# Long convolution between the gated products of a one-core transformer kernel

## What is computed

```python
proj = u @ w_in[i]
y_a = conformer_conv_branch(proj[..., OFF_CONV:OFF_Z], ...) @ w_conv_out[i]
y_b = ssd_branch(...) @ w_ssd_out[i]
y_c = swa_branch(...) @ w_attn_out[i]
gates = sigmoid(proj[..., OFF_GATE:IN_COLS] + gate_bias[i])
merged = gates[0] * y_a + gates[1] * y_b + gates[2] * y_c

def conformer_conv_branch(u, dw_w, dw_b, ln_g, ln_b):
    a, gate = jnp.split(u, 2, axis=-1)
    h = a * jax.nn.sigmoid(gate)
    h = causal_depthwise_conv(h, dw_w, dw_b)   # 31 taps, per feature
    h = layer_norm(h, ln_g, ln_b)
    return jax.nn.silu(h)
```

## Time and profile before

| | us |
|---|---|
| median of 3 runs | 2835.9 |
| lowest, highest | 2833.11, 2838.72 |
| the profiled execution | 2840.97 |
| its span on the core | 2838.9 |

### The profile page before, as it was taken

One profiled execution on the slowest core, in us unless ns is written; L12 is line 12 of the kernel. 1 busy time (PEld: TensorE's weight loads), 2 busy tenths in 40 slices (PEclk: granted clock), 3 DMA queues, 4 the chain that ended last, 5 costly groups with the idle time before them and its releaser, 6 DMA issues.

```text
span 2838.9 us, 53058 instructions
## 1 busy us (share of the span) xinstructions
PE 2747.1 (97%) x22084; PEld 2404.2 (85%) x22084; DVE 1436.5 (51%) x2761; ACT 1185.8 (42%) x2115; POOL 1473.2 (52%) x809
## 2 busy tenths in 40 slices
PE   7999999988889999999999999999999999999999
PEld 5888888767778888889888897899998898898999
DVE  3777226645554666504666124443174776612570
ACT  3222235334444322224222236644445665555553
POOL 2444434443323444443444433388885476597797
PEclk9999999999999999999999999999999999999999
DMA  6565323210001455433555326365564343354465
GB/s 271 188 209 201 106 88 97 92 60 3 3 4 32 149 183 186 150 95 122 190 171 182 111 76 123 102 198 187 171 186 134 97 149 120 103 180 149 141 194 164
DMA packets 105974, 380.98 MB, mean 134 GB/s; under 512 B 11367, under 2 KB 16648, under 8 KB 104456
## 3 DMA queue, kind: packets, MB, share of 16 engines
q1 hardware_dynamic: 87304, 310.47, 35.2%
q10 hardware_dynamic: 18432, 67.12, 6.7%
HBM read 373.34 MB, written 4.19 MB: 133 GB/s over the span
## 4 chain that ended last, share of the span: by engine, by line
PE 89%; DVE 4%; POOL 3%; ACT 3%; issue 2%; DMA 1%; SPq 0%; DVEq 0%; ACTq 0%
PE bank L233 24%; PE bank L234 24%; PE bank L235 24%; POOL weights_lo L226 2%; PE bank L1075 2%; PE upper_banks L233 1%; PE upper_banks L234 1%; PE upper_banks L235 1%; PE upper_banks L1880 1%; PE upper_banks L1863 1%; PE bank L1172 1%; PE bank L1854 1%; PE upper_banks L1091 1%; PE upper_banks L1052 1%; PE upper_banks L1202 1%
## 5 line engine op out<-in xcount | busy, mean ns | idle before, releaser
L226 POOL TENSOR_TENSOR weights_lo<-weights_landing,weights_hi 128x1024 fp32r<-128x1024 f32 x554 | 1339.3, 2424 | 1152.5 <-ACT weights_hi L216 1151.5
L216 ACT ACTIVATE weights_hi<-weights_landing 128x1024 fp32r<-128x1024 f32 x554 | 587.3, 1061 | 1162.7 <-PE bank L235 1048.9
L233 PE MATMUL bank<-normed_hi,weights_lo 128*128 128x256 f32 (+1 forms) x2776 | 926.7, 334 | 3.0 <-DVE normed_lo L736 1.7
L234 PE MATMUL bank<-normed_lo,weights_hi 128*128 128x256 f32 (+1 forms) x2776 | 919.2, 331 | 0.0
L235 PE MATMUL bank<-normed_hi,weights_hi 128*128 128x256 f32 (+1 forms) x2776 | 917.7, 331 | 0.0
L233 PEld LDWEIGHTS bank<-normed_hi,weights_lo 128*128 128x128 f32 x2776 | 522.8, 188 | 69.3 <-issue 4.4
L235 PEld LDWEIGHTS bank<-normed_hi,weights_hi 128*128 128x128 f32 x2776 | 522.9, 188 | 56.3
L234 PEld LDWEIGHTS bank<-normed_lo,weights_hi 128*128 128x128 f32 x2776 | 523.0, 188 | 55.9
L233 PE MATMUL bank<-hidden_hi,weights_lo 128*128 128x256 f32 (+1 forms) x1026 | 340.8, 332 | 0.0
L234 PE MATMUL bank<-hidden_lo,weights_hi 128*128 128x256 f32 (+1 forms) x1026 | 340.1, 331 | 0.0
L235 PE MATMUL bank<-hidden_hi,weights_hi 128*128 128x256 f32 (+1 forms) x1026 | 339.7, 331 | 0.0
(11 more groups left out here) (473 smaller groups left out, 3711.7 us busy)
## 6 DMA issues: line engine op xcount, KB each, us to landing
weights_landing<-w_up SPq DMA_DIRECT2D x176, 512.0 KB, 3.6
ada_rows<-w_ada_rows ACTq DMA_DIRECT2D x128, 512.0 KB, 4.4
weights_landing<-w_down SPq DMA_DIRECT2D x88, 512.0 KB, 3.5
weights_landing<-w_dn SPq DMA_DIRECT2D x33, 512.0 KB, 3.6
weights_landing<-w_mlp_up SPq DMA_DIRECT2D x32, 512.0 KB, 3.6
weights_landing<-w_mlp_down SPq DMA_DIRECT2D x32, 512.0 KB, 3.5
weights_landing<-w_gate SPq DMA_DIRECT2D x24, 512.0 KB, 3.5
weights_landing<-w_xbc SPq DMA_DIRECT2D x24, 512.0 KB, 3.5
```

What stands on the lines that cost most here:

```text
L216: k.nc.scalar.activation(k.WH[:, u % SLOTS, :], k.W[:, u % LANDS, :], ACT.Copy).then_inc(*k.AC.mark(("unit hi", u)))
L226: k.nc.gpsimd.tensor_tensor(k.WL[:, u % SLOTS, :], k.W[:, u % LANDS, :], k.WH[:, u % SLOTS, :].bitcast(F32), ALU.subtract).then_inc(*k.PO. ...
L233: nc.tensor.matmul(out, ll, rh, start=start, stop=False, skip_group_check=True)
L234: nc.tensor.matmul(out, lh, rl, start=False, stop=False, skip_group_check=True)
```

## The change

The gated products now use four banks (0 to 3) in turn. The convolution uses bank 7 alone. Its steps stand between the products: 6 steps behind the second product, 10 behind each of the third to seventh, 150 behind the last, then two after each of nine parts of the query projection and none after its last two. That makes 6 + 50 + 150 + 18 = 224 steps, seven tiles, ahead of the attention; one tile stays behind it. Each convolution tile waits for its own product only. The value projection no longer waits for four tiles of the convolution, and the attention's second output waits for tile 6 in place of tile 4. Nothing is computed differently.

```diff
@@ window_project_pe
-        pe.wait_ge(*k.DV.after("conv", 3))
@@ spread_heads_pe, outputs
-            pe.wait_ge(*k.DV.after("conv", CONV_APART))
+            pe.wait_ge(*k.DV.after("conv", KT - 2))
@@ long_conv
-        y = k.B[7 if at == CONV_APART else 6 + at % 2][:, 0:LAT]
-        dve.wait_ge(*k.DV.after("glu", "ev", KT - 1))
+        y = k.B[7][:, 0:LAT]
+        dve.wait_ge(*k.DV.after("glu", "ev", at))
@@ glu_pe
-    freed = lambda n: None if n < 8 else k.AC.after("glu", "sig", (n - 8) // 2) if n % 2 else k.DV.after("glu", "ev", (n - 8) // 2)
-    linear(k, pe, "glu", "w_glu", 2 * KT, KT, both2(k), LAT, freed, norm_ready(k, "norm mix"), first=4, banks=8)
+    freed = lambda n: None if n < 4 else k.AC.after("glu", "sig", (n - 4) // 2) if n % 2 else k.DV.after("glu", "ev", (n - 4) // 2)
+    linear(k, pe, "glu", "w_glu", 2 * KT, KT, both2(k), LAT, freed, norm_ready(k, "norm mix"), first=4)
@@ glu_dve
+        if 1 <= n < KT - 1:
+            take(conv, 10 if n > 1 else 6)
@@ gates_pe
-                       k.AC.after("glu", "sig", KT - 4 + n // 2) if n % 2 else k.DV.after("glu", "ev", KT - 4 + n // 2))
+                       k.AC.after("glu", "sig", KT - 2 + n // 2) if n % 2 else k.DV.after("glu", "ev", KT - 2 + n // 2))
@@ dve_program
-    glu_dve(k, dve)
     conv = long_conv(k, dve)
-    take(conv, 4 * (CONV + 1))
-    window_project_dve(k, dve, attn, lambda n: take(conv, 3 if n < KT + 2 else 2))
+    glu_dve(k, dve, conv)
+    take(conv, 150)
+    window_project_dve(k, dve, attn, lambda n: take(conv, 2 if n < KT + 1 else 0))
...
-    take(conv, 3 * (CONV + 1))
+    take(conv, CONV + 1)
```

More of the change, by code:

```diff
@@ L2065 @@
 CONV = 31
-CONV_APART = 4
 def both2(k):
@@ L2117, in glu_act, with glu_dve @@
                 act.wait_ge(*k.DV.after("glu", "ev", n // 2 - 2))
-            k.nc.scalar.activation(k.sigs[:, n // 2 % 2, :], k.B[n % 8][:, 0:LAT], ACT.Sigmoid).then_inc(*k.AC.mark(("glu", "sig", n // 2)))
-def glu_dve(k, dve):
+            k.nc.scalar.activation(k.sigs[:, n // 2 % 2, :], k.B[n % 4][:, 0:LAT], ACT.Sigmoid).then_inc(*k.AC.mark(("glu", "sig", n // 2)))
+def glu_dve(k, dve, conv):
     for n in range(KT):
         dve.wait_ge(*k.AC.after("glu", "sig", n))
-        k.nc.vector.tensor_tensor(k.gl[:, n, :], k.sigs[:, n % 2, :], k.B[2 * n % 8][:, 0:LAT], ALU.mult).then_inc(*k.DV.mark(("glu", "ev", n)))
+        k.nc.vector.tensor_tensor(k.gl[:, n, :], k.sigs[:, n % 2, :], k.B[2 * n % 4][:, 0:LAT], ALU.mult).then_inc(*k.DV.mark(("glu", "ev", n)))
+        if 1 <= n < KT - 1:
+            take(conv, 10 if n > 1 else 6)
 def gates_pe(k, pe):
     freed = lambda n: (k.AC.after("gates", "ev", n - 4) if n >= 4 else
-                       k.AC.after("glu", "sig", KT - 4 + n // 2) if n % 2 else k.DV.after("glu", "ev", KT - 4 + n // 2))
+                       k.AC.after("glu", "sig", KT - 2 + n // 2) if n % 2 else k.DV.after("glu", "ev", KT - 2 + n // 2))
     linear(k, pe, "gates", "w_gate", 24, KT, both2(k), LAT, freed)
```

## The result

| | before | with the change |
|---|---|---|
| median of 20 runs, us | 2836.6 | 2839.63 |
| lowest, highest | 2830.76, 2843.52 | 2835.16, 2847.57 |
| span of the profiled execution | 2838.9 | 2837.0 |

The ratio is 1.0014, with a 95% interval from 1.0008 to 1.0021: 2 to 6 us slower, some 4 us, which is inside the 0.2% taken as no change. A second series of 7 runs of the change, with 29 of the kernel before beside them, gave a ratio of 1.0026 (1.0015 to 1.0037), some 7 us; the two intervals overlap between 1.0015 and 1.0021. The forecast was +4.4 us and 2840.3 us.

What follows compares the result with a forecast made beforehand. PE was taken as the bound, busy 97% of the span with 89% of the chain that ended last. Terms 4.9 + 2.3 - 2.8 = +4.4 us gave a median of 2840.3 us, range 2835.0 to 2845.0.

Steps and rivals of the forecast that it cites:

- The wait: Gated products: with four banks PE stops before the fifth tile until the first product is done, +4.9 us (4.5 to 5.2).
- The chain: Gated products: weight DMA, weight copy, table load of 1.28 us and sigmoid set the first product's end, about 2041.3.
- The clock behind it: Gated products after PE's stop: 5.2 us at 1.2 GHz, losing 0.45 per microsecond, +2.3 us (0 to 2.8).
- the rival in which it holds: Gated products: the clock holds through PE's stop, sum +2.1 us, 2838.0 us; chance 15%.
- Ten steps between products, 150 under the gates: Gated products and gates: convolution steps fit, 5.55 us within 5.65 and 3.3 us left under the gates; cost 0.
- The attention's start: Seventh reciprocal to first maximum: seven fewer multiply-adds stand between, -2.8 us (-2.3 to -3.4).
- The walk: Attention's start, step by step from the seventh reciprocal at 2182.86: first maximum at 2186.4 in place of 2189.22.
- One tile behind the attention: Behind the attention: DVE reaches the xbc convolution 32.7 us earlier and waits for PE; gain 0.
- The slower rival: Gated products: the lower clock lasts 13.7 us behind the stop, costing 6.2 us, sum +8.3, 2844.2 us; chance 12%.
- The faster rival: Attention's start runs at the full clock, up to 6.2 us less, sum -1.8, 2834.1 us; chance 5%.

Runs made afterwards that it cites:

- early table load: The changed kernel with one small sigmoid on a constant ahead of the gated products' weight copies: 2839.69 us, ratio 1.0011.
- matmuls in the wait: The changed kernel with ten matmuls of constants ahead of the fifth gated-product tile: 2842.78 us, ratio 1.0015; measured again, 2837.71 us, ratio 1.0008.
- earlier steps alone: The kernel before, eight banks kept, with 14 steps of the fifth convolution tile moved under the gates: 2834.65 us, ratio 0.9989.

## Why the prediction was right

**The wait.** Forecast +4.9, bounds 4.5 to 5.2; measured 5.3 and 5.1 in the change (5.42 and 5.24 less 0.11), 5.0 with four banks alone. The first of these is 0.1 beyond the upper bound. The chain was right, as the early table load shows. The small miss has a source in the first trace: the first four tiles took 11.19 us where the earlier trace rows had 11.30, and the first product came 16.14 us after the first matmul in place of 15.82; in the second it was 15.95.

**The clock behind it.** Forecast +2.3, bounds 0 to 2.8, from one wait of 4.14 us elsewhere. The low stretches in new work were 4.2, 3.4, 6.0 and 3.4 us (the change, its second run, four banks, early table), and the stretch behind the fifth tile was longer by 2.0, 1.6, 2.8 and 1.6 us, at like spacing of the matmuls. A loss of 0.45 per microsecond nearly holds: 4.2 x 0.45 = 1.9. With the wait filled the loss is 0.1. The clock fell in all four executions that had the wait open, in two of them only 0.2 and 1.3 us after PE had started again. So the rival in which it holds did not come true in any. By the Trainium skill's rule (TensorE: Matmul & The Clock Gate, Terms), a half, the estimate is 3.0 for the 6.0 us of four banks alone and 2.1 for 4.2 us. The traces have 2.8 and 2.0, between that and 0.45.

**Ten steps between products, 150 under the gates.** Forecast 0, measured 0: from the fifth tile to the values the six-bank kernel takes 106.40 us with the steps and the kernel before with the attention's matmuls takes 106.40 without. The slack under the gates was 1.95 us, not 3.3: the closer spacing of PE's matmuls took 0.7 of it (the steps' start moved by 3.8 us, the reciprocal by 3.2), and the sign change of the sinks (0.84 us at 2152.89), which I had left out, most of the rest.

**The attention's start.** Forecast -2.8, bounds -2.3 to -3.4; measured -3.2 and -2.9, -3.2 to -3.0 with six banks, -3.1 and -2.5 with matmuls in the wait, and -2.1, just beyond the bound, with the earlier steps alone. The walk had the last spread at the lower clock. In the change the clock was still full there, so the spread took 0.6 us to the scores in place of 1.05.

**One tile behind the attention.** Forecast 0, measured 0: 53.40 against 53.41 us to the sums. DVE idles 32.5 us.

**The slower rival** (the lower clock stays for long) named the right thing in the wrong place. Behind the wait it was never over 6.0 us. At the attention it was 3.4 to 20.5 us, and it differed between the two executions of each of the three kernels without matmuls there that were profiled twice (6.8 and 17.1, 17.1 and 13.7, 3.4 and 13.7). **The faster rival** put at most 6.2 us on it; at the full clock the stretch is 35.5 us, so the lower clock and the short waits that went with it cost 2.3 us in the kernel before and up to 4.7 in others. Holding it needed more than the change brought.

**The sum.** 5.3 + 2.0 - 3.2 = +4.1 from the first trace and 5.1 + 1.6 - 2.9 = +3.8 from the second, beside the +4 of the ratio. The clock's terms are taken at like spacing of the matmuls; against the 107.42 us of before's own trace the first would be 1.0. The sums also leave out the stretch from the maximum to z, which had -0.1 in the first trace and +2.3 in the second (40.11 against 37.85). With it the second trace has +6.1, beside the 7 us of its series.

So each mechanism was as forecast, and the closeness of the total is in part luck: the wait was 0.2 to 0.4 larger, the clock 0.3 to 0.7 smaller and the gain at the attention 0.1 to 0.4 larger than said, errors that cancel in part. The low stretch at the attention, for which the range allowed 1 us, added 2.3 in the second execution and nothing in the first.

## What to carry to other kernels

Before giving up a buffer, look for the one consumer that starts late. Here the ring of four banks was long enough for every tile but the first one behind a group of four, where a table load and a weight landing held back the first sigmoid, and with six banks there was no wait. A wait of PE can cost more than its length: here waits of 3.8 to 5.3 us brought 1.6 to 2.8 us more through the lower clock, in four executions of four. Read the stretch at the lower clock from a wait of like length in the same trace. Where PE's short waits sit together, take away the work that causes them first and then fill what is left with matmuls into a free bank: in the series that had all three, the ratios were 0.9989 and 0.9990 for either alone and 0.9977 for both.

## What was not expected of the hardware

The same dense tiles run at one of two spacings, with the granted clock at 1.00 in both. In the kernel before, one weight unit takes 2.83 us in the gated products and gates, 117.8 ns a matmul; in the change it takes 2.80, 116.7 ns, as ACT's weight copies show, which follow PE's units:

```profile
2054.94 1.06 ACT L216 ACTIVATE weights_hi<-weights_landing 128x1024 fp32r<-128x1024 f32 x1 [1.47 <-PE bank L235]
...
2057.74 1.06 ACT L216 ACTIVATE weights_hi<-weights_landing 128x1024 fp32r<-128x1024 f32 x1 [1.74 <-PE bank L235]
...
2060.54 1.06 ACT L216 ACTIVATE weights_hi<-weights_landing 128x1024 fp32r<-128x1024 f32 x1 [1.47 <-PE bank L235]
```

Over the 912 matmuls from the fifth tile to the values that is 107.42 against 106.40 us. In the stretch to the sums it is 53.91 against 53.40: the three executions with 53.91 had the wider spacing there. Both occur in one execution, and they do not follow the kernel: the same program had 117.8 in one run and 116.7 in its other for three kernels of the table. The stretch of before is therefore to be compared with 106.40 in kernels of the closer spacing. What sets it was not tried.

The length of the low stretch at the attention's start, 3.4 to 20.5 us in the profiled executions, is as unsteady; it may be part of why single runs of one kernel spread over 10 us, which was not shown. With six banks and five short matmuls of constants there was none, in either of two executions.
